# A hybrid attention layer: odd diff heads take their row tiles in another order, and the score steps form eleven PSUM batches for twelve

## What is computed

```
h   = RMSNorm_pre(x)
u   = h @ W_in                      # 1024 x 4096
A   = 4 differential heads: softmax(q0 k0) - lam * softmax(q1 k1), each causal, times v (128 wide)
B   = 8 MoBA heads of 64; at 512 rows and blocks of 256 this is plain causal attention
both: logits * scale + relative-position bias; output * SiLU(gate)
y   = concat(A, B) @ W_out
out = x + RMSNorm_post(y)
```

## Time and profile before

| | before |
|---|---|
| median of 3 runs | 254.22 us (254.18 to 254.46) |
| the profiled execution's own time | 254.23 us |
| its span, first to last instruction | 252.4 us |
| TensorE busy | 245.6 us, 97% |
| VectorE busy | 177.0 us, 70% |
| ScalarE busy | 143.0 us, 57% |
| mean granted TensorE clock | 0.997 |

### The profile page before, as it was taken

The page is one execution under the profiler, slowest core; times in us unless marked ns, Lnnn a source line. Parts: engine busy times, 40 slices in busy tenths (PEclk is TensorE's granted clock), DMA queues, the critical chain, the costliest instruction groups (busy, mean ns, idle before and its releaser), DMA issues.

```text
span 252.4 us, 4450 instructions
## 1 busy us (share of the span) xinstructions
PE 245.6 (97%) x1567; PEld 123.2 (49%) x1567; DVE 177.0 (70%) x393; ACT 143.0 (57%) x336; POOL 32.7 (13%) x74
## 2 busy tenths in 40 slices
PE   8999999999999999999999999999999999999991
PEld 6454444445444554544455444454444444555570
DVE  2998585587478688868877767977787896835313
ACT  4777565375356666574677595667565665611110
POOL 1329300000000320041031033000000000111101
PEclk9999999999999999999999999999999999999998
DMA  6978979605656545544935644568849869982422
GB/s 242 366 245 173 310 251 371 218 28 135 106 160 163 180 114 130 140 163 112 203 103 136 137 161 119 136 189 184 174 103 201 209 157 170 202 203 43 125 86 83
DMA packets 59674, 42.47 MB, mean 168 GB/s; under 512 B 45808, under 2 KB 46072, under 8 KB 59652
## 3 DMA queue, kind: packets, MB, share of 16 engines
q1 hardware_dynamic: 59636, 42.18, 63.5%
q10 hardware_dynamic: 16, 0.00, 0.0%
HBM read 29.04 MB, written 2.13 MB: 123 GB/s over the span
## 4 chain that ended last, share of the span: by engine, by line
PE 97%; DVE 1%; DVEq 0%; POOLq 0%; issue 0%; ACT 0%; POOL 0%; ACTq 0%
PE unit_ps L578 72%; PE score_ps L634 6%; PE o_ps L655 5%; PE unit_ps L608 4%; PE unit_ps L589 3%; PE unit_ps L615 2%; PE unit_ps L543 1%; PE score_ps L536 1%; PE score_ps L709 1%; PE unit_ps L709 1%; DVE area L1058 0%; DVE gates L956 0%; DVEq L180 0%; POOLq L180 0%; ACT junk L732 0%
## 5 line engine op out<-in xcount | busy, mean ns | idle before, releaser
L578 PE MATMUL unit_ps<-area,w_hi 128*128 128x512 f16 x256 | 76.2, 379 | 0.0
L788 ACT ACTIVATE arena<-arena,negmax 128x512 f32<-128x512 f32 (+3 forms) x64 | 35.4, 554 | 49.5 <-DVE negmax L985 49.4
L578 PE MATMUL unit_ps<-w_hi,area 128*128 128x512 f16 x192 | 60.3, 379 | 0.0
L578 PE MATMUL unit_ps<-area,w_lo 128*128 128x512 f16 x128 | 48.5, 379 | 0.0
L578 PEld LDWEIGHTS unit_ps<-area,w_hi 128*128 128x128 f16 x256 | 24.1, 98 | 27.2 <-issue 1.1
L578 PE MATMUL unit_ps<-w_lo,area 128*128 128x512 f16 x96 | 36.4, 379 | 0.0
L985 DVE CUSTOM_DVE_ANT_0 arena<-score_ps,strips 128x512 f32<-128x512 f32 (+3 forms) x64 | 28.6, 485 | 9.2 <-PE score_ps L634 9.2
L882 DVE SCALAR_TENSOR_TENSOR w_lo<-stage,g_cols,w_hi 128x512 f16<-128x512 f32 x32 | 24.2, 755 | 11.3 <-ACT w_hi L746 11.2
L578 PEld LDWEIGHTS unit_ps<-w_hi,area 128*128 128x128 f16 x192 | 18.8, 98 | 21.9 <-DVE w_lo L888 0.7
L745 ACT ACTIVATE w_hi<-stage,g_cols 128x512 f16<-128x512 f32 x32 | 22.7, 711 | 7.3 <-DMA stage<-in_w_in_dram 7.3
L884 DVE SCALAR_TENSOR_TENSOR w_lo<-stage,g_cols,w_hi 128x512 f16<-128x512 f32 x32 | 24.8, 777 | 0.0
(11 more groups left out here) (106 smaller groups left out, 357.7 us busy)
## 6 DMA issues: line engine op xcount, KB each, us to landing
stage<-in_w_in_dram SPq DMA_DIRECT2D x32, 512.0 KB, 4.3
stage<-in_w_out_dram SPq DMA_DIRECT2D x8, 512.0 KB, 4.2
arena<-in_x_dram SPq DMA_DIRECT2D x4, 512.0 KB, 5.2
strips<-bias_rows SPq DMA_DIRECT2D x4, 512.0 KB, 4.7
stage<-in_x_dram SPq DMA_DIRECT2D x4, 512.0 KB, 4.7
out_dram<-area SPq DMA_DIRECT2D x3, 512.0 KB, 2.7
strips<-bias_rows SPq DMA_DIRECT2D x1, 1024.0 KB, 7.8
pt<-arena SPq DMA_TRANSPOSE x32, 3.1
```

Of the source, the lines that this page charges most:

```text
L578: last = nc.tensor.matmul(bank, a, b, start=(k == 0 and n == 0), stop=(k == KT - 1 and n == 2))
L788: nc.scalar.activation(probs[:, i % 2, m, 0:n], probs[:, i % 2, m, 0:n], ACT.Exp, bias=negmax[:, i, m:m + 1], scale=-1.0, accum_out=sums[: ...
```

## The change

Diff heads with an odd number take their row tiles as 1, 3, 0, 2 where they took 3, 0, 2, 1, and the list of batches is another one. No other line changes. Steps 4 to 7 then have t = 1, 3, 0, 2 (before 3, 0, 2, 1), and so have steps 12 to 15. Every other step stays.

```
-    STEPS = [(0, t, c) for c in range(CHUNKS) for t in (3, 0, 2, 1)]
+    STEPS = [(0, t, c) for c in range(CHUNKS) for t in ((1, 3, 0, 2) if c % 2 else (3, 0, 2, 1))]
...
-    BATCHES = [[0, 1], [2, 3], [4, 5, 6], [7, 8, 9], [10, 11], [12, 13, 14], [15, 16, 17, 18, 19, 20],
-               [21, 22, 23], [24, 25], [26, 27], [28, 29], [30, 31]]
+    BATCHES = [[0, 1, 2], [3, 4, 5], [6, 7, 8], [9, 10, 11, 12], [13, 14, 15], [16, 17, 18, 19, 20, 21],
+               [22, 23, 24], [25, 26], [27, 28], [29, 30], [31]]
```

## The result

| | before | changed |
|---|---|---|
| median of 22 runs each | 254.25 us (253.58 to 255.26) | 255.23 us (253.77 to 256.76) |
| the profiled execution's own time | 254.23 us | 254.85 us |
| its span | 252.4 us | 253.1 us |
| TensorE busy | 245.6 us | 245.8 us |
| mean granted TensorE clock | 0.997 | 0.997 |

The ratio of the changed kernel's time to that of the kernel before is 1.0034, with a 95% interval of 1.0022 to 1.0047: some 0.9 us slower, where 0.8 was forecast. The profiled execution is 0.62 us slower than that of before, less than the 0.98 by which the medians differ; some executions lose more, which the end of this document comes back to.

What follows compares the result with a forecast made beforehand. TensorE, busy 97% of the span, was taken to bound the kernel. 254.23 less 0.18 for one batch fewer plus 0.94 for a transpose wait gave 254.99, say 255.0 us; range 254.0 to 255.4.

Steps and rivals of the forecast that it cites:

- The batch: TensorE's entry to and exit from score batches: twelve become eleven, 0.09 us each way, 0.18 us less.
- TensorE 1.02 us early in slots 28 and 30: Scores moved between slots and fewer batches bring TensorE to values(26) and values(28) 1.02 us earlier, values(28) at 211.77.
- The place and kind of the loss: Slot 30, values(28): TensorE waits once for the DMA transpose of step 28, 0.94 us, bounds 0 and 1.34.
- When the transpose lands: Step 28's transpose into pt: issued at 207.01, 5.7 us on its way, landing at 212.71.
- p_lo(28) and with it the transpose is 0.32 later: VectorE, ScalarE and DMA chain in slots 25 to 29 starts at values(23), 0.32 us later, and moves p_lo(28) equally.
- If it takes the same 5.7: Step 28's transpose was assumed to keep its earlier 5.7 us from issue to landing, not the 4.3 of step 29's.
- The first rival: Slot 30: step 28's transpose takes under 4.76 us, TensorE doesn't wait, 254.05 us, within 0.2%; chance 0.26.
- What was late next: After slot 30's wait, scores and logits of steps 30 and 31 were costed at nothing; failed cover would delay values(30).

Runs made afterwards that it cites:

- the old pairs: Changed kernel with MoBA steps batched 16-20, 21-23, 24-25, 26-27, 28-29, 30-31, new row-tile order kept, eleven batches: ratio 0.9992 against the kernel before, repeated 1.0002.
- the control: Kernel before with 24 fewer waits on TensorE's queue, twelve batches: 254.26 against 254.14 us, ratio 1.0005.
- the shifted pairs without the new order: Kernel before, old row-tile order, MoBA steps batched as in the changed kernel (21 alone, 22-24, 25-26, 27-28, 29-30, 31 alone): 255.05 against 254.12 us, ratio 1.0044.
- The run with fewer waits: Changed kernel with 24 fewer waits on TensorE's queue, scores waiting for q and k units only in a chunk's first step: 254.24 us, ratio 1.0002.
- the second run of the changed kernel: The changed kernel itself, unaltered, measured once more beside the others on the same chip: 255.46 us, ratio 1.0049 against the kernel before.
- the kernel before with the fetch earlier: Kernel before with 16 more already fulfilled waits on TensorE's queue in slots 16 to 18: 254.47 us, ratio 1.0011.

## Why the prediction was right

- **The batch.** Forecast 0.18 us less, at 0.09 each way. The changed kernel has one such pair fewer, and enters at the same price (0.31, as before). The medians can't show so little, but the traces can, when the first 15 us with their early waits are left out. From the start of the first L608 matmul to that of TensorE's last, the kernel before takes 231.26 us and the old pairs, with one batch fewer, 231.05 (the control, twelve batches with fewer waits, takes 231.26 again):

```profile
15.36 0.38 PE L608 MATMUL unit_ps<-w_hi,area 128*128 128x512 f16 x1
...
246.62 0.27 PE L709 MATMUL score_ps<-w_hi,q_lo 128*128 128x256 f16 x1
```
```profile
15.03 0.38 PE L608 MATMUL unit_ps<-w_hi,area 128*128 128x512 f16 x1
...
246.08 0.27 PE L709 MATMUL score_ps<-w_hi,q_lo 128*128 128x256 f16 x1
```

  That is 0.21 for 0.18, right. The profiled 253.68 of the old pairs is lower by 0.55, but 0.33 of it lies in the first 15 us and has nothing to do with the change. The changed kernel takes 232.01 (15.24 to 247.25), 0.75 more than before: 0.18 less for the batch, 0.82 for the wait, and 0.12 for the loss in slot 28 that the last point names.
- **TensorE 1.02 us early in slots 28 and 30.** Forecast: values(28) wanted at 211.77. By its predecessor it was wanted at 211.75. The count of score matmuls is right, but that the two times agree to 0.02 is luck: the profiled execution started the slots 0.12 us earlier than that of before (15.24 for 15.36), so that v(26) came 1.18 early (198.70 for 199.88) and v(23) 0.17 late for 0.32, and the loss in slot 28 took the 0.12 back.
- **The place and kind of the loss.** One wait of TensorE for the transpose of step 28 in slot 30, 0.94 forecast, 0.82 measured. The old pairs and the shifted pairs without the new order show that it takes the shift. The run with fewer waits shows that it takes a held-up transpose besides. The prediction had one too, but another, as the next point tells. From 0.94 to 0.82: the transpose landed 0.28 earlier than forecast, and the way from the landing to the matmul, taken as 0, was some 0.14.
- **When the transpose lands.** Forecast 212.71, measured 208.14 + 4.3 = 212.4. This came out of two terms, both mis-sized, that cancelled. "p_lo(28) and with it the transpose is 0.32 later": it was 1.44 later. "If it takes the same 5.7": it took 4.3. The step that failed is the reason given for the second, "the order on SP stays, and the load of x follows as closely". It did stay, and the transpose was fast nevertheless. The 5.7 was no property of this transfer and its neighbours; it was 4.3 plus 1.4 us of a fetch that happened to fall on it, at 209.8. In the changed kernel that fetch came at 213.9 only, and the one ahead of it at 193.1 for 194.4. This one had met the transpose of step 26 before, which landed 1.7 us ahead of its use all the same (193.01 + 5.1, for 199.88); now it fell on the transposes of the gated heads, which are links of the very chain that leads to step 28. The chain got 1.1 us that the forecast hadn't, and the transfer at its end lost 1.4. That the two nearly cancel is luck.
- **The first rival** in the prediction had the wait vanish if the transpose took less than 4.76 us. It took 4.3, and the wait was there, so its condition was not enough: it held the chain for fixed. With fewer waits on the queue both hold (4.6 for the gated head, 4.3 for step 28), TensorE doesn't wait, and the time is 254.24, within the 0.2% that the rival named.
- **What was late next.** Costed at nothing in slots 31 to 33, rightly: no wait there. Not seen was slot 28: the bank of an output unit comes free behind the same late chain (the matmul starts 0.05 to 0.06 us after L908's end), 0.24 us in the second run of the changed kernel (0.27 less 0.03) and 0.12 in its first profile, where the pair starts at 199.20 and 199.35.

## What to carry to other kernels

Before shifting work on the engine that bounds the kernel, list for each instruction there that takes a transfer how long its input lay ready; the earlier the engine arrives, the more of these margins it eats, and here 1.02 us of earliness against 0.40 of margin cost more than the batch saved. A duration read once from a trace is no constant if anything without a place in the program can fall on it: look for a neighbour of the same size, and ask what was in flight. Where a loss hangs on where something falls, a few instructions without work move it, and that is a cheap test.

## What the runs showed of the hardware

A fetch of TensorE's instructions, one 16 KB packet every 12 to 29 us here, that falls into a DMA transpose from SBUF to SBUF most often holds it up: 5.7 for 4.5 us, 5.7 for 4.3, 5.1 for 3.8. By how much depends on where in the transfer it falls. The thirteen traces have 416 transposes into pt, and each can be held against the median of those of its kind (diff or MoBA, same row tile) that had no fetch between issue and landing. A fetch within 0.3 us of the issue cost 0 to 0.3 us (5 cases), one at 0.3 to 0.7 us 0 to 0.6, mostly 0.4 to 0.6 (11), one at 0.7 to 1.2 us 0.3 to 1.6 (11), and one at 1.2 to 3.4 us 0.3 to 2.0, with 1.3 as the median (36); two fell later still, near the landing, with 0.5 and 1.0. So in the kernel before with the fetch earlier, step 28's took only 4.8 for 4.3, with the fetch 0.8 us after its issue. Of the 351 transposes without a fetch, 323 were within 0.3 us of their median; the 22 that were over it by more than 0.5 are all of steps 3, 6 and 22. With 16 instructions more or 24 fewer the fetch moved, and with it the hold-up, to another transpose. The fetch isn't tied to an exact instruction: the one that met step 28 before came 4 us later in the changed kernel, which has the same 3306, and why is not shown. What the two share (a ring, the engine that writes, an order between reads) is not shown by these runs, and a fetch between two transposes cost nothing that could be seen. It may be part of why the changed kernel's loss varies, as the waits for early transfers are: its 22 runs went from 253.8 to 256.8 us, those of before from 253.6 to 255.3.
